# The MLP's two projections as units of 1024 cubed, each by seven half-size products, with GpSimd forming the operands' sums

## The chip, the core and the metric

The kernel runs on one core of a Trainium2 chip. The metric is the device time of one execution in microseconds (us), the median of three runs: 3414.43 us, with 3413.43 and 3418.71 as the other two. The engines are TensorE (PE; its weight loads are PEld), VectorE (DVE), ScalarE (ACT), GpSimd (POOL), and SyncE (SP), whose queue issues the DMA transfers. All data are float32.

## The reference, cut to what matters

Two transformer blocks run one after the other on 1024 tokens of width 1024. The change touches the very end, the squared-ReLU MLP of the second block, and the final norm only in its order:

```python
def squared_relu_mlp(xn, w_ff1, w_ff2):
    h = jax.nn.relu(jnp.einsum('bsd,df->bsf', xn, w_ff1))
    return jnp.einsum('bsf,fd->bsd', h * h, w_ff2)
...
        xn = rmsnorm(h, norm_mlp_g[l])
        h = h + squared_relu_mlp(xn, w_ff1[l], w_ff2[l])
    return rmsnorm(h, norm_final_g)
```

`xn` is 1024 x 1024, `w_ff1` 1024 x 4096, `w_ff2` 4096 x 1024: eight products of 1024 x 1024 by 1024 x 1024.

## The kernel before, in words

Every float32 matrix is cut in two parts: `high`, the value rounded to the format that TensorE multiplies (`F32R`), and `low`, the rest. A product is three matmuls, high x high, high x low and low x high; low x low is left out. A matmul is 128 x 128 by 128 x 512.

Each stage is one call of `project` (L462). It streams its weight through a `Stream` (L401): pieces of 128 x 2 x 512 (512 KB) are loaded to `m_w_raw` by SP (L427), ACT rounds each to its high part (L513), DVE subtracts for the low part (L517), both into `m_w_cut`, two pieces deep. A piece feeds eight PSUM tiles with six matmuls each (L626), 48 matmuls in all.

The MLP (`mlp_second`, L4112) takes the hidden width in eight chunks of 512. `up(j)` makes chunk j of the hidden layer from `mlp_high` and `mlp_low`, the normed rows, cut once for all chunks; ACT takes a PSUM tile with ReLU and squares it (L4134, L4135), DVE cuts it again (L4139, L4140). `down(j)` multiplies the chunk by its rows of `w_ff2`, and DVE adds the PSUM tile to `x` (L2022). The order is up(0), up(1), down(0), up(2), down(1), and so on: 3072 matmuls, 384 for each 1024-cubed product. While it goes on, GpSimd has nothing to do.

The stage ahead, `m2_out`, is a `project` too (128 x 3 matmuls). As it starts, SP loads the residual `x` (4 MB) and the gain vector, and behind them the third weight piece (`fetch`). At its end `RowsTurned` (L1401) norms rows 0 to 3: ACT squares and takes roots (L1432, L1435), DVE scales (L1446), PE transposes (L1452), ACT and DVE cut (L1457, L1461). Rows 4 to 7 follow between the first tiles of the MLP. At the end `FinalNorm` works in the same manner on each row tile as its last addition is done (L4179, L4202), and SP stores it.

What sets the order is each engine's own instruction list, with semaphores between them; engines also meet at the border of two stages.

## Time and profile before

| what | value |
|---|---|
| median of the runs | 3414.43 us (3413.43 to 3418.71) |
| span of the profiled execution | 3412.1 us |
| PE busy | 3092.3 us (91%), 14840 matmuls |
| DVE busy | 1392.4 us (41%) |
| ACT busy | 935.4 us (27%) |
| POOL busy | 188.4 us (6%) |
| share of the MLP's matmuls (L626, `mlp_ps`) in the chain that ended last | 20% |
| the MLP's matmuls, first and last start | 2698.0 and 3400.6 us |

The chain is followed back from the last instruction to what released each step. PE being busy says only that matmuls were in flight: whether it runs at its full rate is read from how far apart matmuls start and from the granted clock. Lines (L626) are those of the kernel before.

### The profile page before, as it was taken

The numbers are of one execution on the slowest core, as the hardware profiler recorded it, in microseconds if no ns is written. First come the engines' busy times: TensorE is split into PE (matmuls) and PEld (weight loads), VectorE is DVE, ScalarE is ACT, GpSimd is POOL, SyncE is SP. The second block draws the span as 40 slices with busy tenths as digits, with TensorE's granted clock in tenths as the row PEclk, the third lists the DMA queues.
The fourth block names the chain that finished last, engine by engine and source line by source line (L and its number), as shares of the span: only waits on it lengthen the run. The fifth ranks groups of instructions, "written<-read, shape, count | busy, mean of one in ns | idle before, by whom it ended". The sixth has DMA issues, their size and how long they took to land. (4 is left out here: it accounts for less than half of the span.)

```text
span 3412.1 us, 36355 instructions
## 1 busy us (share of the span) xinstructions
PE 3092.3 (91%) x14840; PEld 2322.7 (68%) x14840; DVE 1392.4 (41%) x2134; ACT 935.4 (27%) x1484; POOL 188.4 (6%) x247
## 2 busy tenths in 40 slices
PE   7997778999998888878774999999999999999998
PEld 7886754667776674322222977888887788888887
DVE  3126846884434343111115646521225433333334
ACT  3532335663324221000004131021321322222221
POOL 0001023110000001111112000000000000000000
PEclk9998889999999999998996999999999999999999
DMA  3111000003220048999995132111112121111112
GB/s 99 47 50 7 7 14 1 1 1 118 83 78 7 31 187 343 420 421 420 416 396 203 34 83 71 50 50 47 38 59 99 50 62 50 50 50 49 44 49 80
DMA packets 141158, 372.17 MB, mean 109 GB/s; under 512 B 45952, under 2 KB 59904, under 8 KB 115008
## 3 DMA queue, kind: packets, MB, share of 16 engines
q1 hardware_dynamic: 130640, 349.06, 28.3%
q0 software_dynamic: 9216, 16.80, 1.3%
q10 hardware_dynamic: 1152, 4.19, 0.3%
q8 instruction: 108, 1.77, 0.2%
q14 instruction: 42, 0.34, 0.0%
HBM read 354.80 MB, written 32.83 MB: 114 GB/s over the span
## 5 line engine op out<-in xcount | busy, mean ns | idle before, releaser
L517 DVE TENSOR_TENSOR m_w_cut<-m_w_raw,m_w_cut 128x1024 fp32r<-128x1024 f32 (+1 forms) x153 | 162.9, 1065 | 794.8 <-ACT m_w_cut L513 794.1
L513 ACT ACTIVATE m_w_cut<-m_w_raw 128x1024 fp32r<-128x1024 f32 (+1 forms) x153 | 142.3, 930 | 1010.5 <-PE mlp_ps L626 521.3
L626 PE MATMUL mlp_ps<-mlp_high,m_w_cut 128*128 128x512 f32 x1024 | 315.7, 390 | 1.1 <-PEq L572 1.1
L626 PE MATMUL mlp_ps<-m_w_cut,mlp_hidden_high 128*128 128x512 f32 x1024 | 315.2, 389 | 0.0
L2963 PE MATMUL ffn_ps<-moe_wgu,moe_rowsT 128*64 128x512 f32 x1024 | 240.0, 623 | 53.0 <-issue 26.5
L626 PEld LDWEIGHTS mlp_ps<-mlp_high,m_w_cut 128*128 128x128 f32 x1024 | 191.8, 188 | 40.9 <-issue 1.3
L626 PEld LDWEIGHTS mlp_ps<-m_w_cut,mlp_hidden_high 128*128 128x128 f32 x1024 | 192.2, 188 | 39.9
L2963 PEld LDWEIGHTS ffn_ps<-moe_wgu,moe_rowsT 128*64 128x64 f32 x1024 | 77.8, 143 | 194.6 <-issue 165.2
L626 PE MATMUL mlp_ps<-mlp_low,m_w_cut 128*128 128x512 f32 x512 | 199.2, 389 | 0.0
L626 PE MATMUL mlp_ps<-m_w_cut,mlp_hidden_low 128*128 128x512 f32 x512 | 199.2, 389 | 0.0
L2999 DVE TENSOR_TENSOR moe_hid<-ffn_ps,moe_gated 128x256 f32<-128x256 f32 x32 | 13.6, 425 | 414.5 <-ACT moe_gated L3011 414.5
L626 PE MATMUL m_cv_ps<-m_high,m_w_cut 128*128 128x512 f32 x512 | 162.4, 399 | 7.6 <-DVE m_w_cut L517 2.6
L626 PE MATMUL m_gates_ps<-m_high,m_w_cut 128*128 128x512 f32 x512 | 157.8, 389 | 1.1 <-PEq L572 1.1
L2984 PE MATMUL ffn_logitsT_ps<-moe_wd,moe_hidT 128*64 128x512 f32 x512 | 118.6, 605 | 18.0 <-DVE moe_hidT L3005 18.0
L626 PE MATMUL mix_in_ps<-mix_high,mix_w_cut 128*128 128x512 f32 x384 | 118.7, 390 | 0.1
L626 PEld LDWEIGHTS m_cv_ps<-m_high,m_w_cut 128*128 128x128 f32 x512 | 96.2, 191 | 31.0 <-DVE m_w_cut L517 7.7
L2022 DVE TENSOR_TENSOR x<-mlp_ps,x 128x512 f32<-128x512 f32 x128 | 86.9, 689 | 68.9 <-PE mlp_ps L626 68.9
L626 PEld LDWEIGHTS m_gates_ps<-m_high,m_w_cut 128*128 128x128 f32 x512 | 96.0, 188 | 21.3 <-issue 1.5
L626 PE MATMUL mix_in_ps<-mix_w_cut,mix_high 128*128 128x512 f32 (+1 forms) x384 | 109.6, 367 | 0.9 <-PEq L286 0.9
L626 PEld LDWEIGHTS mlp_ps<-mlp_low,m_w_cut 128*128 128x128 f32 x512 | 96.1, 188 | 20.0
L626 PEld LDWEIGHTS mlp_ps<-m_w_cut,mlp_hidden_low 128*128 128x128 f32 x512 | 96.1, 188 | 20.0
L517 DVE TENSOR_TENSOR mix_w_cut<-mix_w_raw,mix_w_cut 128x512 fp32r<-128x512 f32 (+1 forms) x47 | 31.4, 667 | 189.1 <-ACT mix_w_cut L513 189.0
(566 smaller groups left out, 5900.0 us busy)
## 6 DMA issues: line engine op xcount, KB each, us to landing
moe_wgu<-in_moe_w_gate_dram SPq DMA_DIRECT2D x64, 1024.0 KB, 20.0
moe_wgu<-in_moe_w_up_dram SPq DMA_DIRECT2D x64, 1024.0 KB, 25.3
moe_wd<-in_moe_w_down_dram SPq DMA_DIRECT2D x64, 1024.0 KB
m_w_raw<-in_w_ff_dram SPq DMA_DIRECT2D x68, 512.0 KB, 3.6
m_w_raw<-in_w_in_dram SPq DMA_DIRECT2D x48, 256.0 KB, 2.8
mix_w_raw<-in_w_in_dram SPq DMA_DIRECT2D x40, 256.0 KB, 2.6
m_w_raw<-in_w_in_dram SPq DMA_DIRECT2D x20, 512.0 KB, 3.6
x_w_raw<-in_x_w_kv_dram SPq DMA_DIRECT2D x16, 512.0 KB, 3.6
```

What stands on the lines that cost most here:

```text
L513: nc.scalar.activation(part(s, 0).bitcast(F32R), raw(s), ACT.Copy).then_inc(high_ready, 1)
L517: nc.vector.tensor_tensor(part(s, 1).bitcast(F32R), raw(s), part(s, 0), ALU.subtract).then_inc(low_ready, 1)
L626: ins = nc.tensor.matmul(ps[:, place, :r.shape[-1]], l, r, start=(k == 0 and sw is high and wh == 0), stop=(k == job.nk - 1 and sw is low))
L2022: return nc.vector.tensor_tensor(x[:, b, at], ps, x[:, b, at], ALU.add)
L2963: ins = self.nc.tensor.matmul(self.ps_h[r, i].rearrange("p (i n) -> p i n", i=2), self.rowsT[:, i, k, r], self.wgu[:, w * self.parts + h, ...
L2984: ins = self.nc.tensor.matmul(self.ps_y[r, half], self.hidT[:, i, k, r], self.wd[:, w * self.parts + h, k, half * CH:(half + 1) * CH], sta ...
L2999: self.nc.vector.tensor_tensor(self.hid[:, b % self.small], self.ps_h[:, b % self.small, EH:], self.gated[:, b % self.small], ALU.mult).th ...
```

## The change

The eight 1024-cubed products become eight `Unit`s in the order up 0, down 0, up 1, down 1, ... (an up unit makes 1024 hidden columns, a down unit adds its product to `x`). Each unit is done by the scheme of seven products of 512-cubed (Winograd's form of Strassen's). The operands A (activations) and B (weights) are taken as 2 x 2 blocks, and beside them four sums of each are formed:

- S1 = A21 + A22, S2 = S1 - A11, S4 = A12 - S2, S3 = A11 - A21
- T1 = B12 - B11, T2 = B22 - T1, T3 = B22 - B12, T4 = B21 - T2
- products in this order: A11 B11, A12 B21, S2 T2, S4 B22, S1 T1, S3 T3, A22 T4. They accumulate in two groups of four PSUM banks, and `TAKES` says to which of the four output blocks a bank's content is added after each product.

GpSimd makes the sums, 16 instructions of 128 x 1024 in a unit (each block in two halves). A product is two *pieces* g (its two halves in the contracted dimension), so 14 pieces in a unit and 112 in all; a piece is four PSUM tiles of six matmuls. Nothing is cut ahead of time any more: for every piece ACT rounds the A half and the B half (`high_a`, `high_w`), and DVE subtracts for the low parts (`low_a`, `low_w`, which read two operands in SBUF), into rings three pieces deep. ACT and DVE cut piece g+2 as soon as piece g-1 has been multiplied, and then take the PSUM tiles of piece g where it ends a product: in an up unit ACT copies the first content of a block and DVE adds the others (16 additions in a unit), in a down unit DVE makes all (32). ReLU and square run once a block is complete (`square`). The final norm of rows 0 to 3 moves into the last unit. The weight blocks lie in four slots of 1 MB; six half blocks are loaded in `m2_out` behind the residual, the B22 block of unit 0 only after row 7 has been turned, since its slot holds the rows' room until then.

```diff
@@ -4099,63 +4099,419 @@
-            mlp_jobs, mlp_rows, final, load_gain = mlp_second(c, a, x, base, flat(small))
+            mlp_rows, begin_mlp = mlp_second(c, a, x, base)
...
-            project(c, "mlp", stream, mlp_jobs, side=mlp_rows, tail=final)
+            mlp_rows.sevens.run()
+PRODUCTS = (("A11", "B11", 0, True), ("A12", "B21", 1, True), ("S2", "T2", 0, False), ("S4", "B22", 1, True),
+            ("S1", "T1", 0, False), ("S3", "T3", 1, True), ("A22", "T4", 1, False))
+TAKES = ((("11", True),), (("11", False),), (("21", True),), (("12", True),), (("12", False), ("22", True)),
+         (("22", False),), (("21", False),))
+SUMS = (("T1", 0), ("T2", 0), ("T1", 1), ("T2", 1), ("S1", 0), ("S2", 0), ("S1", 1), ("S2", 1),
+        ("S4", 0), ("S4", 1), ("T3", 0), ("S3", 0), ("T3", 1), ("S3", 1), ("T4", 0), ("T4", 1))
+USES = {name: q for q, names in enumerate(PRODUCTS) for name in names[:2]}
+FINAL = ("11", "12", "22", "21")
+SLOTS = {"B11": 0, "B21": 1, "B12": 2, "B22": 3, "T1": 0, "T2": 4, "T3": 2, "T4": 4}
+RING = 3
...
+    def high_a(self, act, g):
+        u, q, h = self.piece(g)
+        name = PRODUCTS[q][0]
+        if g >= RING:
+            act.wait_ge(self.products, 4 * (g - RING + 1))
+        if name[0] == "A":
+            self.act_ready(act, u, name, h)
+            src = self.a_block(u, name, h)
+        else:
+            act.wait_ge(self.summed, self.sum_done(u, name, h))
+            src = self.a_sum(name, h)
+        self.nc.scalar.activation(self.a_part(g, 0).bitcast(F32R), src, ACT.Copy).then_inc(self.a_high, 1)
...
+    def low_a(self, dve, g):
+        u, q, h = self.piece(g)
+        name = PRODUCTS[q][0]
+        src = self.a_block(u, name, h) if name[0] == "A" else self.a_sum(name, h)
+        dve.wait_ge(self.a_high, g + 1)
+        self.nc.vector.tensor_tensor(self.a_part(g, 1).bitcast(F32R), src, self.a_part(g, 0),
+                                     ALU.subtract).then_inc(self.a_low, 1)
...
+    def sum(self, pool, u, name, h):
+        nc = self.nc
+        out = self.w_slot(name, h) if name[0] == "T" else self.a_sum(name, h)
+        mine = lambda n: pool.wait_ge(self.summed, self.sum_done(u, n, h))
+        came = lambda n: pool.wait_ge(self.arrived[SLOTS[n]][h], 16 * (u + 1))
+        if name == "T1":
+            came("B12")
+            pool.wait_ge(self.w_low, self.split(u, "B11", h))
+            l, r = self.w_slot("B12", h), self.w_slot("B11", h)
+        elif name == "T2":
+            came("B22")
+            mine("T1")
+            if u:
+                pool.wait_ge(self.w_low, self.split(u - 1, "T4", h))
+            l, r = self.w_slot("B22", h), self.w_slot("T1", h)
+        elif name == "T3":
+            mine("T1")
+            l, r = self.w_slot("B22", h), self.w_slot("B12", h)
+        elif name == "T4":
+            mine("T2")
+            pool.wait_ge(self.w_low, self.split(u, "T2", h))
+            l, r = self.w_slot("B21", h), self.w_slot("T2", h)
+        elif name == "S1":
+            self.act_ready(pool, u, "A22", h)
+            self.act_ready(pool, u, "A21", h)
+            if u:
+                pool.wait_ge(self.a_low, self.split(u - 1, "S1", h))
+            l, r = self.a_block(u, "A21", h), self.a_block(u, "A22", h)
+        elif name == "S2":
+            mine("S1")
+            if u:
+                pool.wait_ge(self.a_low, self.split(u - 1, "S3", h))
+            l, r = self.a_sum("S1", h), self.a_block(u, "A11", h)
+        elif name == "S4":
+            mine("S2")
+            pool.wait_ge(self.a_low, self.split(u, "S2", h))
+            l, r = self.a_block(u, "A12", h), self.a_sum("S2", h)
+        else:
+            mine("S4")
+            pool.wait_ge(self.a_low, self.split(u, "S4", h))
+            l, r = self.a_block(u, "A11", h), self.a_block(u, "A21", h)
+        nc.gpsimd.tensor_tensor(out, l, r, ALU.add if name == "S1" else ALU.subtract).then_inc(self.summed, 1)
...
+        for block, first in TAKES[q]:
+            if (first and up) != (mine == "scalar"):
+                continue
+            for tile in range(4):
+                ps, at = self.ps[:, 4 * PRODUCTS[q][2] + tile], self.c_block(u, block, tile)
+                eng.wait_ge(self.products, 4 * g + tile + 1)
+                if mine == "scalar":
+                    if len(TAKES[q]) > 1:
+                        eng.wait_ge(self.added, adds + tile + 1)
+                    nc.scalar.activation(at, ps, ACT.Copy).then_inc(self.copied, 1)
+                    continue
...
+                nc.vector.tensor_tensor(at, ps, at, ALU.add).then_inc(self.added, 1)
...
+    def square(self, act, u, q):
...
+            self.nc.scalar.activation(at, at, ACT.Relu).then_inc(self.squared, 1)
+            act.wait_ge(self.squared, self.final_done(u, block, h))
+            self.nc.scalar.activation(at, at, ACT.Square).then_inc(self.made, 1)
...
+    def multiply(self, pe, g, tile):
+        u, q, h = self.piece(g)
+        _, _, banks, opens = PRODUCTS[q]
+        a, w = [[part(g, i).bitcast(F32R) for i in range(2)] for part in (self.a_part, self.w_part)]
+        if h == 0:
+            self.bank_free(pe, u, q, tile)
+        cols = slice(tile * P, (tile + 1) * P)
+        for k in range(2):
+            for n, (x, y) in enumerate(((0, 0), (0, 1), (1, 0))):
+                l, r = (w[y][:, k, cols], a[x][:, k]) if self.units[u].up else (a[x][:, k, cols], w[y][:, k])
+                ins = self.nc.tensor.matmul(self.ps[:, 4 * banks + tile], l, r, start=(opens and h == k == n == 0),
+                                            stop=(h == k == 1 and n == 2), skip_group_check=True)
+        ins.then_inc(self.products, 1)
+    def begin(self, sp):
+        for name in ("B11", "B21", "B12"):
+            for h in range(2):
+                self.load(sp, 0, name, h)
...
+                @block.sync
+                def _(sp):
+                    for u in range(len(units)):
+                        if u:
+                            for h in range(2):
+                                sp.wait_ge(self.w_low, self.split(u - 1, "T1", h))
+                                self.load(sp, u, "B11", h)
+                            for h in range(2):
+                                sp.wait_ge(self.summed, self.sum_done(u - 1, "T4", h))
+                                self.load(sp, u, "B21", h)
+                        else:
+                            sp.wait_ge(rows.turned, NT)
+                        for h in range(2):
+                            if u:
+                                sp.wait_ge(self.w_low, self.split(u - 1, "B22", h))
+                                sp.wait_ge(self.summed, self.sum_done(u - 1, "T3", h))
+                            self.load(sp, u, "B22", h)
+                        if u:
+                            for h in range(2):
+                                sp.wait_ge(self.w_low, self.split(u - 1, "T3", h))
+                                self.load(sp, u, "B12", h)
+                    final.last_stores(sp, self.a_low, 14 * last)
+                @block.gpsimd
+                def _(pool):
+                    c.clear()
+                    for u in range(len(units)):
+                        for name, h in SUMS:
+                            self.sum(pool, u, name, h)
+                @block.scalar
+                def _(act):
+                    self.high_a(act, 1)
+                    self.high_w(act, 1)
+                    for g in range(n):
+                        if g + 2 < n:
+                            self.high_a(act, g + 2)
+                            self.high_w(act, g + 2)
+                        for m in {0: (4, 5), 1: (6, 7)}.get(g, ()):
+                            rows.high(act, m)
+                        u, q, h = self.piece(g)
+                        if g and h == 0:
+                            u_was, q_was, _ = self.piece(g - 1)
+                            if units[u_was].up and any(not first for _, first in TAKES[q_was]):
+                                self.square(act, u_was, q_was)
+                        if h and units[u].up:
+                            self.take(act, u, q, "scalar")
+                        if u == last and q == 4 and h:
+                            final.roots(act, range(NT // 2), self.added, self.adds[self.at(u, 4)])
+                    final.roots(act, range(NT // 2, NT), self.added, self.adds[self.at(last, 6)] - NT // 2)
+                @block.vector
+                def _(dve):
+                    rows.scale(dve, 4)
+                    self.low_a(dve, 1)
+                    self.low_w(dve, 1)
+                    for g in range(n):
+                        if g == 0:
+                            rows.scale(dve, 5)
+                        if g + 2 < n:
+                            self.low_a(dve, g + 2)
+                            self.low_w(dve, g + 2)
+                        if g == 0:
+                            rows.scale(dve, 6)
+                            rows.scale(dve, 7)
+                        u, q, h = self.piece(g)
+                        if h:
+                            self.take(dve, u, q, "vector")
+                        if u == last and q == 5:
+                            for m in range(2 * h, 2 * h + 2):
+                                final.scale(dve, m)
+                    for m in range(NT // 2, NT):
+                        final.scale(dve, m)
+                @block.tensor
+                def _(pe):
+                    for g in range(n):
+                        pe.wait_ge(self.a_low, g + 1)
+                        pe.wait_ge(self.w_low, g + 1)
+                        if g == 2:
+                            pe.wait_ge(rows.split, NT)
+                        for tile in range(4):
+                            self.multiply(pe, g, tile)
+                            if tile in (1, 3) and g < 2:
+                                m = 4 + 2 * g + tile // 2
+                                if m >= 6:
+                                    pe.wait_ge(rows.split, m - 1)
+                                rows.turn_row(pe, m)
...
+    def beside_sums(self, act, added, before):
+        self.sevens.high_w(act, 0)
+        super().beside_sums(act, added, before)
+        self.sevens.high_a(act, 0)
+    def after_sum(self, dve, b):
+        if b is None:
+            self.scale(dve, 3)
+            self.sevens.low_w(dve, 0)
+            self.sevens.low_a(dve, 0)
+        elif 2 <= b < 5:
+            self.scale(dve, b - 2)
```

GpSimd's list, at the MLP. Before, the stage has only its branch; now the sums of each unit stand there (`mlp_raw` holds weight blocks, `mlp_sums` the S sums; the lines shown are unit 0).

```order
-L594 UNCONDITIONAL_BRANCH x2
+L594 UNCONDITIONAL_BRANCH
+L4392 UNCONDITIONAL_BRANCH
+L4285 TENSOR_TENSOR mlp_raw<-mlp_raw 128x1024 x4
+L4285 TENSOR_TENSOR mlp_sums<-mlp_normed 128x1024
+L4285 TENSOR_TENSOR mlp_sums<-mlp_sums,mlp_normed 128x1024
+L4285 TENSOR_TENSOR mlp_sums<-mlp_normed 128x1024
+L4285 TENSOR_TENSOR mlp_sums<-mlp_sums,mlp_normed 128x1024
+L4285 TENSOR_TENSOR mlp_sums<-mlp_normed,mlp_sums 128x1024 x2
```

The order is T1, T2, T1, T2, then S1, S2, S1, S2, S4, S4, and T3, S3, T3, S3, T4, T4 behind them.

VectorE's list in the MLP before: one subtraction for each weight piece, eight additions to `x` from PSUM for each down job, and the cut of the hidden tiles.

```order
L517 TENSOR_TENSOR m_w_cut<-m_w_raw,m_w_cut 128x1024 x4
L4139 CAST mlp_hidden_high_17665<-mlp_squares 128x512
L4140 TENSOR_TENSOR mlp_hidden_low_17666<-mlp_squares,mlp_hidden_high_17665 128x512
L2022 TENSOR_TENSOR x<-mlp_ps,x 128x512 x8
```

VectorE's list now, from a down unit's first additions on: pieces 3 and 4, then 5 and 6, and so on.

```order
L4313 TENSOR_TENSOR x<-mlp_ps,x 128x512 x4
L4235 TENSOR_TENSOR mlp_a_ring<-mlp_sums,mlp_a_ring 128x1024
L4241 TENSOR_TENSOR mlp_w_ring<-mlp_raw,mlp_w_ring 128x1024
L4235 TENSOR_TENSOR mlp_a_ring<-mlp_sums,mlp_a_ring 128x1024
L4241 TENSOR_TENSOR mlp_w_ring<-mlp_raw,mlp_w_ring 128x1024
L4313 TENSOR_TENSOR x<-mlp_ps,x 128x512 x4
```

The cut of the hidden tiles is gone, and two subtractions for each 24 matmuls have come in place of one for each 48.

TensorE's list now, from the start of the MLP.

```order
L4351 MATMUL mlp_ps<-mlp_a_ring,mlp_w_ring 128x512 x12
L1452 MATMUL mlp_ps<-ident,mlp_raw 128x128 x8
L4351 MATMUL mlp_ps<-mlp_a_ring,mlp_w_ring 128x512 x288
L4351 MATMUL mlp_ps<-mlp_w_ring,mlp_a_ring 128x512 x336
L4351 MATMUL mlp_ps<-mlp_a_ring,mlp_w_ring 128x512 x336
```

The first two of these lines stand there four times (rows 4 to 7); then follow the rest of unit 0 and the seven other units of 336 matmuls each.

## Rows read from the trace of the kernel before

**Rows 1.** The chain of waits from 2560 us on: start, duration, what.

```profile
2718.26 675.95 PE mlp_ps L626 x2982
```

**Rows 2.** Stretches: length, busy time of each engine (instructions), PE clock, DMA share, GB/s.

```profile
3000.00:3100.00 100.00, 100.00 (x443) 82.81 (x442) 36.15 (x50) 19.27 (x25) 0.00 (x0) 1.00 0.16 48
```

**Rows 3.** Timeline of PE at the MLP's end: start, duration, instruction.

```profile
3396.07 0.62 PE L626 MATMUL mlp_ps<-m_w_cut,mlp_hidden_high 128*128 128x512 f32 x2
...
3400.15 0.62 PE L626 MATMUL mlp_ps<-m_w_cut,mlp_hidden_high 128*128 128x512 f32 x2
```

**Rows 4.** Groups of instructions, 2600 to 3412 us: busy, mean ns; idle before.

```profile
L517 DVE TENSOR_TENSOR m_w_cut<-m_w_raw,m_w_cut 128x1024 fp32r<-128x1024 f32 x74 | 90.7, 1225 | 432.0 <-ACT m_w_cut L513 431.6
L2022 DVE TENSOR_TENSOR x<-mlp_ps,x 128x512 f32<-128x512 f32 x128 | 86.9, 689 | 68.9 <-PE mlp_ps L626 68.9
L513 ACT ACTIVATE m_w_cut<-m_w_raw 128x1024 fp32r<-128x1024 f32 x74 | 78.3, 1058 | 579.8 <-PE mlp_ps L626 521.3 <-PE m_out_ps L626 46.3 <-DMA m_w_raw<-in_w_out_dram 10.5
```

**Rows 5.** Timeline of POOL, 1825 to 1862 us.

```profile
1832.61 2.35 POOL L3259 TENSOR_TENSOR x<-x,m_t 128x1024 f32<-128x1024 f32 x1 [1.22 <-DVE x L3252]
...
1853.62 2.35 POOL L3259 TENSOR_TENSOR x<-x,m_t 128x1024 f32<-128x1024 f32 x1 [3.25 <-DVE x L3252]
```

**Rows 6.** Timeline of DVE in the same stretch.

```profile
1832.65 3.39 DVE L346 SCALAR_TENSOR_TENSOR m_t<-x,m_norm_rstd,m_t 128x1024 f32<-128x1024 f32 x1
...
1851.00 1.28 DVE L346 SCALAR_TENSOR_TENSOR m_t<-x,m_norm_rstd,m_t 128x1024 f32<-128x1024 f32 x1
...
1853.51 1.22 DVE L362 TENSOR_TENSOR m_low<-m_norm_ps,m_high 128x1024 fp32r<-128x1024 f32 x1
```

**Rows 7.** Timeline of POOL, 558 to 592 us.

```profile
561.50 2.33 POOL L907 TENSOR_TENSOR mla_k_low<-mla_kT,mla_k_high 96x1024 fp32r<-96x1024 f32 x1
571.99 1.30 POOL L903 TENSOR_TENSOR mla_q_low<-mla_qT,mla_attn_q_high 96x512 fp32r<-96x512 f32 x1 [8.17 <-ACT mla_attn_q_high L895]
573.25 2.81 POOL L907 TENSOR_TENSOR mla_k_low<-mla_kT,mla_k_high 96x1024 fp32r<-96x1024 f32 x1
```

**Rows 8.** Timeline of DVE in the same stretch.

```profile
572.47 1.38 DVE L983 TENSOR_SCALAR mla_attn_probs<-mla_attn_probs,mla_attn_inv 128x1024 f32<-128x1024 f32 x1
...
575.93 0.75 DVE L983 TENSOR_SCALAR mla_attn_probs<-mla_attn_probs,mla_attn_inv 128x1024 f32<-128x1024 f32 x1
```

**Rows 9.** Stretches at the start of `m2_out`, columns as in rows 2.

```profile
2596.00:2598.00 2.00, 0.00 (x0) 0.00 (x0) 1.97 (x3) 0.00 (x0) 0.00 (x0) 1.00 0.00 0
2598.00:2600.00 2.00, 1.67 (x5) 1.36 (x6) 1.04 (x3) 1.69 (x4) 0.00 (x0) 0.75 0.93 246
2600.00:2602.00 2.00, 2.00 (x6) 1.57 (x5) 2.00 (x5) 2.00 (x5) 0.00 (x0) 0.50 0.65 279
2602.00:2604.00 2.00, 2.00 (x9) 1.59 (x9) 2.00 (x5) 1.53 (x3) 0.00 (x0) 0.90 1.07 459
2606.00:2610.00 4.00, 4.00 (x19) 3.34 (x18) 0.00 (x0) 0.00 (x0) 0.00 (x0) 1.00 0.94 404
```

**Rows 10.** Timeline of ACT in `m2_out`: the third and fourth weight pieces.

```profile
2614.01 1.06 ACT L513 ACTIVATE m_w_cut<-m_w_raw 128x1024 fp32r<-128x1024 f32 x1 [10.48 <-DMA m_w_raw<-in_w_out_dram]
2622.09 1.06 ACT L513 ACTIVATE m_w_cut<-m_w_raw 128x1024 fp32r<-128x1024 f32 x1 [7.02 <-PE m_out_ps L626]
```

**Rows 11.** DMA issues, 2590 to 2700 us: KB each, median us to landing.

```profile
m_w_raw<-in_w_ff_dram SPq DMA_DIRECT2D x3, 512.0 KB, 3.6
```

**Rows 12.** Timeline, 2672 to 2730 us: around the start of the MLP.

```profile
2695.33 2.35 DVE L1461 TENSOR_TENSOR mlp_low<-m_out_ps,mlp_high 128x1024 fp32r<-128x1024 f32 x2 [1.05 <-ACT mlp_high L1457]
...
2698.01 0.70 PE L626 MATMUL mlp_ps<-mlp_high,m_w_cut 128*128 128x512 f32 x2 [1.11 <-PEq L572]
...
2701.82 1.09 PE L1452 MATMUL mlp_ps<-ident,mlp_squares 128*128 128x128 f32 x8 [0.83 <-DVE mlp_squares L1446]
```

**Rows 13.** Groups of instructions, 2600 to 3412 us: the turns in the MLP.

```profile
L1452 PE MATMUL mlp_ps<-ident,mlp_squares 128*128 128x128 f32 x32 | 4.2, 275 | 2.4 <-DVE mlp_squares L1446 2.4
```

**Rows 14.** Timeline of DVE at the end: the last scaling of a row.

```profile
3407.77 1.28 DVE L4202 SCALAR_TENSOR_TENSOR x<-x,s_small,fin_gain 128x1024 f32<-128x1024 f32 x1
```

192 lines of the change are left out of this document (146 added, 46 removed).

## The prediction

> **What bounds the kernel now.** I read the chain of waits first. From 2718.26 us on it is one piece, 675.95 us of the MLP's own matmuls [rows 1]: nothing else is waited for until the final norm. The table of stretches says the same: in 3000 to 3100 us PE is busy throughout at a granted clock of 1.00, with DVE busy 36, ACT 19, POOL 0 and the DMA engines 16% [rows 2]. How fast PE goes is read from the starts: 18 matmuls from 3396.07 to 3400.15 us, 0.2267 us each [rows 3]. So the MLP costs its number of matmuls times 0.2267 us, and everything else is cover. The change takes matmuls away and spends the cover; the question is whether the cover lasts. Times below are against the profiled span of 3412.1 us; the median of the runs is 2.3 us above it.
>
> **Matmuls removed.** 7 instead of 8 half-size products: 8 units x 14 pieces x 24 = 2688 matmuls instead of 3072. 384 x 0.2267 = 87.0 us less. A piece takes 24 x 0.2267 = 5.44 us, a unit 76.2 us. The form of the matmuls does not change.
>
> **What the other engines are given.** In a unit DVE has 28 subtractions at 1.225 us [rows 4] = 34.3 us and 16 additions (up) or 32 (down) at 0.689 [rows 4] = 11.0 or 22.0: 45 or 56 us of 76. ACT has 28 roundings at 1.058 us [rows 4], 30 us, and at most 16 ReLU and square instructions of the same size and 16 half-size copies, 56 us in an up unit. POOL has 16 sums; its nearest rows are the same instruction at the same size, 2.35 us [rows 5], so 37.6 us. Each engine alone fits into 76.2 us. Weight traffic stays the same.
>
> **But DVE and POOL are not alone.** A DVE instruction with two SBUF inputs that starts at 1832.65, 0.04 us behind a POOL sum of 2.35 us, lasts 3.39 us instead of the 1.28 of its like at 1851.00 [rows 5, 6]: it ends 1.08 us after the sum ends (1834.96), so it stood still for the sum's whole length. One whose first input is in PSUM keeps its 1.22 us beside the sum at 1853.62 [rows 5, 6]. So the 28 subtractions cannot run beside the 16 sums, while the additions can. Who comes next when both wait: POOL has two instructions back to back at 571.99 and 573.25; the DVE instruction issued at 572.47 lasts 1.38 us instead of 0.75 [rows 7, 8] and ends at 573.85, and POOL's second lasts 2.81 instead of 2.33, 0.48 longer. The waiter went in between. I take strict turns. The Trainium skill says this in "SBUF — State Buffer", section "Who interferes with whom": the port pair that both use is an exclusive lock for a whole instruction, and a DVE instruction with two SBUF inputs contends with a GpSimd one that reads SBUF. The trace agrees, with the 3.39 us. The skill also speaks against the placement ("GPSIMD Engine Reference", section "When to use GPSIMD": elementwise work on a tile belongs to VectorE); the trace's sum takes 2.35 us to DVE's 1.22 to 1.28.
>
> On the shared port a unit needs 28 x 1.08 + 16 x 2.35 = 68 us of 76.2: enough on average, not everywhere. I walk the lists, t = 0 where PE starts a unit, piece g due at 5.44 g. Cutting g+2 may begin at 5.44 g. POOL begins T1 at about -7 (it waits for the subtraction of B11), and the last of its 16 sums is bound only by its place in the list. With turns (low_a, sum, low_w, sum: 1.1 + 2.35 + 1.1 + 2.35 = 6.9 us for one piece) DVE loses about 1.5 us on each piece while POOL has a backlog. It starts with a lead of 10.9 - 3.5 = 7.4 us (two pieces, less the ACT and DVE time of a cut). In an up unit: piece 2 ready at 9, piece 3 at 16, 4 at 20.6 (due 21.8), 5 at 25.3, 6 at 32.3 (due 32.6), 7 at 39.2 (due 38.1), 8 at 46.2 (due 43.5), then POOL is through at 48.6 and DVE recovers. PE stands still 2.7 us. In a down unit DVE also has 4 additions behind pieces 3, 5 and 7, partly beside sums: piece 7 at 39.9, piece 8 at 49.3, 5.8 us of standstill. 4 x 2.7 + 4 x 5.8 = +34 us.
>
> Bounds: 0 if the sums fall beside additions and idle time (below nothing isn't possible, since a wait can't speed PE up). At the other end every sum delays DVE by its whole 2.35 us and DVE sets the pace: 34.3 + 11.0 + 37.6 = 82.9 and 34.3 + 22.0 + 37.6 = 93.9 us a unit against 76.2, 4 x 6.7 + 4 x 17.7 = 98 us. I keep 34, from the turns of rows 7 and 8.
>
> **The clock after a standstill.** At the start of `m2_out` PE has stood still for the 2.0 us of the first stretch (and a little at both sides); the clock then shows 0.75, 0.50 and 0.90 [rows 9], half level (1.2 GHz) for about 4 us, which costs 2 us. The gap of 1.1 us before the MLP [rows 12] is followed by matmuls at full rate. The long gap of each down unit (about 4 us at piece 8) is of the first kind: 4 x 2 = +8 us; bounds 0 and 16 (all eight units).
>
> **The start of the MLP.** The stage opens when `low_a(0)` is made. DVE's last work before was two cuts from 2695.33, ending at 2697.7 [rows 12]; now ACT rounds A11 behind its last row (+1.06) and DVE subtracts (+1.2), without those cuts: PE begins about 0.8 us later, 2698.8. Then 48 matmuls (10.9 us) and four turns (0.9 us each; [rows 12] has one with 1.09) bring it to 2713.4, and it waits about 1 us for row 7's copy. Here SP may first load B22: it lands 3.6 us later [rows 11], at 2717. T2 is second in POOL's list, so T2, T1, T2, S1, S2 run only from there: 5 x 2.35 = 11.8 us, 2729. Two roundings (2.1) and two subtractions with a sum between them (1.2 + 2.35 + 1.2) make piece 4 ready at 2736. PE has ended piece 3 at 2714.4 + 10.9 = 2725.3: 10.7 us of standstill, and 2 for the clock. Before, PE's waits in this stretch were 2.4 us [rows 13]. 0.8 + 1.0 + 10.7 + 2.0 - 2.4 = +12 us; bounds 6 (first S2 half at once, clock full) and 18.
>
> **`m2_out`.** The third weight piece is loaded behind the residual; ACT got it at 2614.01, and the fourth was released by PE at 2622.09 [rows 10], which is when PE turned to the third. Now 3 MB more lie in front: at the 404 GB/s of 2606 to 2610 [rows 9] 7.8 us, so it comes at 2621.8, is cut at 2624.1, and PE waits 2.0 us, with a little clock: +3 us, bounds 0 and 5.
>
> **The end.** Before, DVE's last scaling ends at 3409.05 [rows 14], 8.0 us after the last matmul (3400.15 + 0.62 + 0.23 = 3401.0), since eight rows are normed there. Now rows 0 to 3 are done before, and DVE has one addition and four scalings of 1.4 us left: 0.7 + 5.6 = 6.3 us. -1.7 us; the last store is the same.
>
> **Sum.** -87.0 + 34 + 8 + 12 + 3 - 1.7 = -32 us: span 3380, median 3382 us.
>
> **The rivals.**
>
> *The sums cost nothing.* POOL fits into DVE's idle half; the 68 of 76.2 us on the port speak for it, the lists' bunching (12 of 16 sums between t = 6 and 48) against it. Standstills and their clock go: -87 + 12 + 3 - 1.7 = -74 us, 3341 us. It would also come out if DVE's second subtraction always went ahead of a waiting sum.
>
> *Slower: DVE becomes the bound.* If a waiting sum goes first whenever it can, and the additions of down units are pushed behind it, the sums add to DVE's work in full: +98 for 34, -87 + 98 + 8 + 12 + 3 - 1.7 = +32 us, 3447 us. It decides from a standstill of (87 - 21) / 8 = 8.2 us a unit. For it: rows 5 and 6, DVE loses the whole length. Against it: it asks that no addition and no idle time ever lies beside a sum, with DVE idle 20 to 31 us of a unit.
>
> *The saving is eaten exactly.* Standstills of 6 to 9 us in both kinds of units, with half clock behind each: -87 + 60 + 16 + 12 + 3 - 2 = +2 us, 3416 us.
>
> **How the numbers follow.** Forecast with its neighbourhood (3358 to 3404) 0.62; sums free 0.20; eaten 0.10, half of it within 0.2%; slower 0.08. 0.2% (6.8 us) is about what a measurement of this kernel can tell from no change. From these: faster 0.85, same 0.05, slower 0.10. The range takes in most of the free case and reaches to the eaten one: 3341 to 3412.
>
> **What would show it.** Right: 2688 matmuls at 0.227 us with PE standing still around pieces 7 and 8 of each unit, longer in down units, waiting for a DVE subtraction; subtractions of 3.4 to 3.6 us beside the usual 1.2; sums of 2.35 us or, behind a subtraction, up to 3.5; one standstill of about 10 us at piece 4 of unit 0, with T2 waiting for a DMA; additions with 0.69 us throughout. Wrong: subtractions that keep 1.2 us beside sums (then the free case), several sums in a row while one subtraction stands (then the slower one), PE waiting for ACT or for a DMA in the later units, or matmuls further apart than 0.227 us without a wait.

## The result, and the profile after

The changed kernel takes 3377.93 us (median of four runs, 3375.55 to 3384.36); the kernel before, on the same chip, 3416.57 us (3413.43 to 3419.94; four runs, with the three known ahead of the prediction among them). The ratio is 0.989, 95% interval 0.9876 to 0.9904: 1.1% faster. The forecast was 3382.0 us, the interval 3341 to 3412. The profiled span is 3373.8 us, against 3412.1.

Where the change acts is measured better between marks of the trace than by spans, since where `m2_out` begins moves by 16 us between executions of kernels that are equal up to there (2593 to 2609 us).

| stretch (us) | before | after | difference | forecast |
|---|---|---|---|---|
| first matmul of `m2_out` to first of the MLP | 99.7 | 103.0 | +3.3 | +3.8 |
| first to last matmul of the MLP | 703.0 | 668.2 | -34.8 | -33.8 |
| last matmul to the end | 11.1 | 9.4 | -1.7 | -1.7 |
| together | 813.8 | 780.6 | -33.2 | -32 |

The other 5.1 us of the span's difference lie ahead of `m2_out`, where nothing was changed. The +3.8 is the +3 of `m2_out` and the 0.8 by which the MLP was to begin later.

The groups of instructions from 2600 us on (busy, mean ns, idle before with its releasers), against [rows 4]:

```profile
L4351 PE MATMUL mlp_ps<-mlp_w_ring,mlp_a_ring 128*128 128x512 f32 x1344 | 316.3, 397 | 18.3 <-issue 13.1 <-DVE mlp_w_ring L4241 2.7 <-DVE x L4313 2.5
L4351 PE MATMUL mlp_ps<-mlp_a_ring,mlp_w_ring 128*128 128x512 f32 x1344 | 313.1, 393 | 21.2 <-issue 13.9 <-DVE mlp_hidden L4313 2.4 <-PEq L572 2.4
L4241 DVE TENSOR_TENSOR mlp_w_ring<-mlp_raw,mlp_w_ring 128x1024 fp32r<-128x1024 f32 x112 | 219.6, 1961 | 0.0
L4285 POOL TENSOR_TENSOR mlp_raw<-mlp_raw 128x1024 f32<-128x1024 f32 x64 | 178.6, 2797 | 892.0 <-POOLq L572 671.0 <-DVE mlp_w_ring L4241 201.1 <-DMA mlp_raw<-in_w_ff_dram 17.9
L4313 DVE TENSOR_TENSOR x<-mlp_ps,x 128x512 f32<-128x512 f32 x128 | 79.8, 679 | 6.0 <-PE mlp_ps L4351 6.0
```

There are 2688 matmuls. The same subtraction that took 1225 ns takes 1961 on average. The T sums (into `mlp_raw`) take 2797 instead of 2350, the S sums 3140 to 3354, and the additions out of PSUM keep their 0.68 us. PE stands still 39.5 us, mostly called "issue": there the semaphores don't show whom it waits for, so the engines' own timelines must. PE in the down unit of the second pair of units, against [rows 2], where it never stopped:

```profile
2955.76 38.24 PE L4351 MATMUL mlp_ps<-mlp_w_ring,mlp_a_ring 128*128 128x512 f32 x168
2994.69 5.68 PE L4351 MATMUL mlp_ps<-mlp_w_ring,mlp_a_ring 128*128 128x512 f32 x24 [0.69 <-DVE mlp_w_ring L4241]
3003.65 4.57 PE L4351 MATMUL mlp_ps<-mlp_w_ring,mlp_a_ring 128*128 128x512 f32 x12 [3.28 <-issue]
```

168 matmuls are seven pieces, then piece 7 is late by 0.69 us, and piece 8 by 3.28. DVE at that time:

```profile
2987.78 3.42 DVE L4235 TENSOR_TENSOR mlp_a_ring<-mlp_sums,mlp_a_ring 128x1024 fp32r<-128x1024 f32 x1
2991.13 3.42 DVE L4241 TENSOR_TENSOR mlp_w_ring<-mlp_raw,mlp_w_ring 128x1024 fp32r<-128x1024 f32 x1
2994.47 2.47 DVE L4313 TENSOR_TENSOR x<-mlp_ps,x 128x512 f32<-128x512 f32 x4
2996.86 3.39 DVE L4235 TENSOR_TENSOR mlp_a_ring<-mlp_sums,mlp_a_ring 128x1024 fp32r<-128x1024 f32 x1
3000.18 3.37 DVE L4241 TENSOR_TENSOR mlp_w_ring<-mlp_raw,mlp_w_ring 128x1024 fp32r<-128x1024 f32 x1
3003.48 1.21 DVE L4235 TENSOR_TENSOR mlp_a_ring<-mlp_sums,mlp_a_ring 128x1024 fp32r<-128x1024 f32 x1
```

And POOL:

```profile
2990.09 3.37 POOL L4285 TENSOR_TENSOR mlp_raw<-mlp_raw 128x1024 f32<-128x1024 f32 x1
2993.43 3.39 POOL L4285 TENSOR_TENSOR mlp_sums<-mlp_hidden 128x1024 f32<-128x1024 f32 x1
2996.76 5.70 POOL L4285 TENSOR_TENSOR mlp_raw<-mlp_raw 128x1024 f32<-128x1024 f32 x2
```

Piece 8 starts when the subtraction at 3000.18 ends (3003.55). While both have work, each instruction of either lasts its own time and the other's (1.08 + 2.3 = 3.4 us): strict turns, as [rows 7, 8] had it. The four additions at 2994.47, out of PSUM, keep 2.47 us beside a sum. The moment POOL's list is empty (3002.46) the subtractions are back at 1.21. The clock behind the standstill (columns as in [rows 2]), against [rows 9]:

```profile
3002.00:3004.00 2.00, 0.35 (x2) 0.34 (x3) 2.00 (x2) 0.42 (x1) 0.47 (x1) 1.00 0.00 0
3004.00:3006.00 2.00, 2.00 (x7) 1.57 (x6) 2.00 (x3) 0.00 (x0) 0.00 (x0) 0.56 0.51 150
3006.00:3008.00 2.00, 2.00 (x7) 1.58 (x6) 2.00 (x4) 0.00 (x0) 0.00 (x0) 0.58 0.67 185
3008.00:3010.00 2.00, 2.00 (x10) 1.63 (x10) 2.00 (x3) 0.00 (x0) 0.00 (x0) 1.00 1.01 359
```

The first twelve matmuls take 4.57 us; at the full clock it would be 12 x 0.2267 and 0.17 for the last one's overlap, 2.9: 1.7 us lost. The other down units have the same standstill of 3.28 us at piece 8, but not always the same clock behind it. The stretch of unit 1 that lies 3.6 to 5.6 us behind its piece 8 (2841.40) is still at half level, its like of unit 3 is nearly over it:

```profile
2845.00:2847.00 2.00, 2.00 (x6) 1.60 (x5) 2.00 (x3) 0.00 (x0) 0.00 (x0) 0.50 0.82 275
3007.00:3009.00 2.00, 2.00 (x9) 1.55 (x9) 2.00 (x4) 0.00 (x0) 0.00 (x0) 0.83 0.73 226
```

Behind 2841.40, 70 matmuls take 18.86 us, 2.8 more than at the full clock; behind 3325.87, 96 take 24.86, 2.9 more; units 3 and 5 lose 1.7 each. PE around the start of the MLP, against [rows 12, 13], and at its end:

```profile
2696.23 4.58 PE L4351 MATMUL mlp_ps<-mlp_a_ring,mlp_w_ring 128*128 128x512 f32 x12 [2.37 <-PEq L572]
...
2713.76 11.16 PE L4351 MATMUL mlp_ps<-mlp_a_ring,mlp_w_ring 128*128 128x512 f32 x48 [1.21 <-ACT mlp_normed L4467]
2735.18 4.99 PE L4351 MATMUL mlp_ps<-mlp_a_ring,mlp_w_ring 128*128 128x512 f32 x15 [10.26 <-issue]
...
3353.26 11.13 PE L4351 MATMUL mlp_ps<-mlp_w_ring,mlp_a_ring 128*128 128x512 f32 x48 [2.54 <-DVE x L4313]
```

The 10.26 us are the first standstill forecast (10.7). What lies behind them, in the timeline of all engines (B22's loads; T2, T1, T2; the first S2; piece 4's first rounding):

```profile
2712.58 0.88 SPq L4195 DMA_DIRECT2D mlp_raw<-in_w_ff_dram  x2
2716.40 7.26 POOL L4285 TENSOR_TENSOR mlp_raw<-mlp_raw 128x1024 f32<-128x1024 f32 x3 [17.89 <-DMA mlp_raw<-in_w_ff_dram]
2726.07 2.34 POOL L4285 TENSOR_TENSOR mlp_sums<-mlp_sums,mlp_normed 128x1024 f32<-128x1024 f32 x1
2728.50 1.06 ACT L4216 ACTIVATE mlp_a_ring<-mlp_sums 128x1024 fp32r<-128x1024 f32 x1 [12.93 <-POOL mlp_sums L4285]
```

POOL waits for B22, then five sums follow one another. PE also waits at piece 12 of each up unit, for PSUM banks. Here is DVE, and then PE, in unit 2:

```profile
2941.66 1.22 DVE L4235 TENSOR_TENSOR mlp_a_ring<-mlp_normed,mlp_a_ring 128x1024 fp32r<-128x1024 f32 x1 [3.61 <-ACT mlp_a_ring L4216]
2943.93 2.47 DVE L4313 TENSOR_TENSOR mlp_hidden<-mlp_ps,mlp_hidden 128x512 f32<-128x512 f32 x4
2944.76 11.16 PE L4351 MATMUL mlp_ps<-mlp_a_ring,mlp_w_ring 128*128 128x512 f32 x48 [0.60 <-DVE mlp_hidden L4313]
```

The additions that free the banks stand behind piece 13's cut in DVE's list, and that cut has waited 3.61 us for ACT, which does ReLU and square from 2936.49 to 2940.67 before it rounds.

### The profile page after: what moved, and what is told of

Same layout as the page of the kernel before. It is cut to its first block and busy times, and to the rows that moved or that the text cites. A ratio compares the mean times of both kernels' runs of the same rounds, so it can differ in the third digit from the quotient of the medians.

```text
span 3373.8 us, 36498 instructions
## 1 busy us (share of the span) xinstructions
PE 3018.7 (89%) x14456; PEld 2254.7 (67%) x14456; DVE 1725.5 (51%) x2218; ACT 1108.4 (33%) x1640; POOL 578.7 (17%) x375
## 5 line engine op out<-in xcount | busy, mean ns | idle before, releaser
L4351 PE MATMUL mlp_ps<-mlp_w_ring,mlp_a_ring 128*128 128x512 f32 x1344 | 316.3, 397 | 18.3 <-issue 13.1
L4351 PE MATMUL mlp_ps<-mlp_a_ring,mlp_w_ring 128*128 128x512 f32 x1344 | 313.1, 393 | 21.2 <-issue 13.9
L4285 POOL TENSOR_TENSOR mlp_raw<-mlp_raw 128x1024 f32<-128x1024 f32 x64 | 178.6, 2797 | 892.0 <-POOLq L572 671.0
L4351 PEld LDWEIGHTS mlp_ps<-mlp_w_ring,mlp_a_ring 128*128 128x128 f32 x1344 | 257.9, 193 | 76.1 <-issue 21.9
L4351 PEld LDWEIGHTS mlp_ps<-mlp_a_ring,mlp_w_ring 128*128 128x128 f32 x1344 | 253.0, 189 | 79.0 <-issue 24.1
L517 DVE TENSOR_TENSOR m_w_cut<-m_w_raw,m_w_cut 128x512 fp32r<-128x512 f32 (+1 forms) x86 | 80.8, 940 | 414.0 <-ACT m_w_cut L513 413.6
L513 ACT ACTIVATE m_w_cut<-m_w_raw 128x512 fp32r<-128x512 f32 (+1 forms) x86 | 71.4, 830 | 490.4 <-PE m_gates_ps L626 190.7
L4241 DVE TENSOR_TENSOR mlp_w_ring<-mlp_raw,mlp_w_ring 128x1024 fp32r<-128x1024 f32 x112 | 219.6, 1961 | 0.0
L4235 DVE TENSOR_TENSOR mlp_a_ring<-mlp_sums,mlp_a_ring 128x1024 fp32r<-128x1024 f32 x64 | 162.6, 2540 | 29.5 <-ACT mlp_a_ring L4216 28.3
L4227 ACT ACTIVATE mlp_w_ring<-mlp_raw 128x1024 fp32r<-128x1024 f32 x112 | 117.1, 1045 | 0.0
```

Source lines behind the costliest of these rows:

```text
L513: nc.scalar.activation(part(s, 0).bitcast(F32R), raw(s), ACT.Copy).then_inc(high_ready, 1)
L517: nc.vector.tensor_tensor(part(s, 1).bitcast(F32R), raw(s), part(s, 0), ALU.subtract).then_inc(low_ready, 1)
L4227: self.nc.scalar.activation(self.w_part(g, 0).bitcast(F32R), self.w_slot(name, h), ACT.Copy).then_inc(self.w_high, 1)
L4235: self.nc.vector.tensor_tensor(self.a_part(g, 1).bitcast(F32R), src, self.a_part(g, 0), ALU.subtract).then_inc(self.a_low, 1)
L4241: self.nc.vector.tensor_tensor(self.w_part(g, 1).bitcast(F32R), self.w_slot(PRODUCTS[q][1], h), self.w_part(g, 0), ALU.subtract).then_inc( ...
L4285: nc.gpsimd.tensor_tensor(out, l, r, ALU.add if name == "S1" else ALU.subtract).then_inc(self.summed, 1)
```

## The experiments

"MLP" below is the stretch from its first to its last matmul in the profiled execution: 703.0 us before, 668.2 after.

**1. Do the sums cost DVE time by reading SBUF, or only by being work for GpSimd?** In the place of each sum GpSimd fills two tiles, 1.17 and 0.96 us, reading nothing. The sums are left out.

```diff
-        nc.gpsimd.tensor_tensor(out, l, r, ALU.add if name == "S1" else ALU.subtract).then_inc(self.summed, 1)
+        self.fill(nc.gpsimd.memset(self.filler[:], 0.0))
+        nc.gpsimd.memset(out, 0.0).then_inc(self.summed, 1)
```

> Each of GpSimd's 128 sums is replaced by two memsets (a spare 128 x 1280 room, then the sum's place), which only write; the sums themselves are left out, so S and T are zero. GpSimd should stay about as busy (some 2.2 us for each) and every semaphore stays. Theory A (the shared read port, as in the prediction): the subtractions of VectorE keep 1.22 us throughout, PE's gaps at pieces 7 and 8 of the units vanish, from the first MLP matmul to the last 668 us become about 633, the time about 3343 us; the gap at piece 4 of unit 0 stays at 8 to 10 us, since it hangs on B22's arrival and five GpSimd steps. Rival B (the length of GpSimd's chain of sums holds PE, whatever they read): gaps stay, 3378 us. Rival C (VectorE's own load is too high without any blocking): gaps stay as well, with subtractions of 1.22 us.

Measured: 3341.8 us (3338.5 to 3348.8), ratio 0.9781 (0.9755 to 0.9806), MLP 631.6 us. Groups of DVE and of POOL from 2700 us on:

```profile
L4242 DVE TENSOR_TENSOR mlp_w_ring<-mlp_raw,mlp_w_ring 128x1024 fp32r<-128x1024 f32 x111 | 135.3, 1219 | 0.0
```

```profile
L4286 POOL MEMSET mlp_filler<- 128x1280 f32 x128 | 149.7, 1170 | 984.6 <-POOLq L572 674.0 <-DVE mlp_w_ring L4242 236.9 <-DVE mlp_a_ring L4236 48.5
```

The subtractions keep 1219 ns beside 272 us of GpSimd's writing, and the standstills at pieces 7 and 8 are gone. So it is the sums that cost it, and not GpSimd being busy or its chain of waits; that it is their reading is the one thing the fills don't share with them, apart from the kind of instruction. At piece 4 of unit 0 PE stands still 6.03 us, not the 8 to 10 expected: the fills are shorter, and the cuts beside them are not held up.

**2. The same from the other side:** from unit 1 on, each sum covers 2 of 512 columns.

```diff
+        few = slice(0, 2 if u else CH)
+        nc.gpsimd.tensor_tensor(out[:, :, few], l[:, :, few], r[:, :, few],
+                                ALU.add if name == "S1" else ALU.subtract).then_inc(self.summed, 1)
```

> From unit 1 on each sum covers only 2 of its 512 columns (the rest of every sum is left out); unit 0 is untouched. Theory A: the same as with writes only, within 3 us, gaps of units 1 to 7 gone, about 3345 us; unit 0's 10.3 us gap stays. Rival B: this one is faster (about 3345), while the one with writes only is not. Rival C: gaps stay, 3378 us.

Measured: 3347.0 us (3345.7 to 3354.6), 0.9802 (0.9778 to 0.9825), MLP 637.6. Unit 0 keeps its 10.18 us at piece 4; units 1 to 7 keep only the waits that are not the sums':

```profile
2735.98 4.60 PE L4353 MATMUL mlp_ps<-mlp_a_ring,mlp_w_ring 128*128 128x512 f32 x10 [10.18 <-issue]
...
2936.49 3.67 PE L4353 MATMUL mlp_ps<-mlp_a_ring,mlp_w_ring 128*128 128x512 f32 x15 [0.61 <-DVE mlp_hidden L4315]
...
3242.90 11.16 PE L4353 MATMUL mlp_ps<-mlp_a_ring,mlp_w_ring 128*128 128x512 f32 x48 [0.61 <-DVE mlp_hidden L4315]
3321.88 12.78 PE L4353 MATMUL mlp_ps<-mlp_w_ring,mlp_a_ring 128*128 128x512 f32 x48 [2.54 <-DVE x L4315]
```

A pair of units takes 153.2 us, against 161.1 in the changed kernel (piece 8 of its down units starts at 2841.40, 3003.65, 3164.79 and 3325.87; the first pair has 162.3): 7.9 us a pair is what the sums cost, with the half clock behind their standstills. Since S and T are wrong or zero in these two runs, it matters that experiment 7, with every sum right, has the same 153.2 us.

**3. The last six sums of a unit spread over later pieces.**

```diff
+PACE = {("T3", 0): 6, ("S3", 0): 7, ("T3", 1): 8, ("S3", 1): 9, ("T4", 0): 9, ("T4", 1): 10}
...
+        pace = PACE.get((name, h))
+        if pace is not None:
+            pool.wait_ge(self.w_low, 14 * u + pace + 1)
```

> Nothing is left out. The last six sums of a unit are held back, so that they spread over pieces 6 to 10 instead of following at once. Theory A with bunching (the port is full only while GpSimd has a backlog): the gaps at pieces 7 and 8 shrink by two thirds or more, the half clock behind those of down units goes, 20 to 26 us less than the changed kernel, about 3354 us. Rival D (the amount of sums is too much for a unit, wherever they stand): the standstill moves to later pieces, within 5 us of 3378.

Measured: 3364.3 us (3363.7 to 3372.9), 0.9854 (0.9829 to 0.9878), MLP 652.0. A miss by 10 us. The standstills at pieces 7 and 8 went, and another came:

```profile
2944.02 12.76 PE L4355 MATMUL mlp_ps<-mlp_a_ring,mlp_w_ring 128*128 128x512 f32 x48 [2.73 <-DVE mlp_hidden L4317]
...
3339.94 12.74 PE L4355 MATMUL mlp_ps<-mlp_w_ring,mlp_a_ring 128*128 128x512 f32 x48 [4.00 <-DVE x L4317]
```

Piece 12 reuses the PSUM banks that DVE empties behind piece 11 (`bank_free`). In unit 2 the cuts at 2922.99 and 2927.45 us last 3.4 us each beside a late sum, so the additions behind piece 9 begin late (2930.79). ACT's copies, ReLU and squares follow them, then the cut of piece 13 (3.61 us of waiting for ACT), and only then the additions that free the banks. I had watched only the cuts.

**4. T1, S1, S2 ahead of T2 in GpSimd's list.**

```diff
-SUMS = (("T1", 0), ("T2", 0), ("T1", 1), ("T2", 1), ("S1", 0), ("S2", 0), ("S1", 1), ("S2", 1),
+SUMS = (("T1", 0), ("T1", 1), ("S1", 0), ("S2", 0), ("T2", 0), ("S1", 1), ("S2", 1), ("T2", 1),
```

> Nothing is left out. GpSimd's list begins T1, T1, S1, S2, T2, S1, S2, T2 instead of T1, T2, T1, T2, S1, S2, S1, S2. Theory A: in unit 0 only T2 waits for B22, so S2's first half is ready at about 2718.3 and T2's at 2720.7 instead of S2's at 2728.4: the 10.3 us gap at piece 4 becomes 2 to 3 us and the half clock after it may go, 8 to 10 us less, about 3369 us; the other units keep 161 us a pair. Rival E (the gap is the row tail itself, ACT's copies and the cut, not the order): less than 3 us change.

Measured: 3385.6 us (3380.1 to 3391.6), 0.9902 (0.9877 to 0.9928), MLP 669.8. A miss. Piece 4 does start 30.8 us after the MLP's start instead of 39.0, but the turning of rows 4 and 5 waits 0.45 and 2.00 us. The 0.45 is in experiment 3 too, where the first twelve matmuls also ran at the full clock; the 2.00 comes from DVE's scaling of row 5, 3.43 us instead of 1.28, beside a T1 sum that in the changed kernel's list waits for B22. And then:

```profile
2741.45 5.71 PE L4351 MATMUL mlp_ps<-mlp_a_ring,mlp_w_ring 128*128 128x512 f32 x24 [0.61 <-issue]
2750.45 12.59 PE L4351 MATMUL mlp_ps<-mlp_a_ring,mlp_w_ring 128*128 128x512 f32 x48 [3.30 <-DVE mlp_w_ring L4241]
2763.96 5.69 PE L4351 MATMUL mlp_ps<-mlp_a_ring,mlp_w_ring 128*128 128x512 f32 x24 [0.92 <-DVE mlp_w_ring L4241]
```

Piece 8 comes 59.9 us after the start, instead of 63.7, and the later units, with the same sums in another order, stand 1.09 + 1.00 + 3.24 us (down) and 0.84 + 0.92 (up). The gain at piece 4 was given back, and more.

**5. The changed kernel once more, and its six first loads behind the third weight piece of `m2_out`.**

> The changed kernel once more, as the yardstick of this call: 3378 us, 161 us for a pair of units, ratio 0.989 to the kernel before.

```diff
                     stream.load(sp, s, pieces[s][2])
+                    if s == 2 and fetch_late:
+                        fetch_late(sp)
```

> Nothing is left out. The six weight loads for the MLP are issued behind m2_out's third weight piece instead of ahead of it. Theory A (the 3 MB in front of the piece make PE wait): the 2.4 to 2.9 us gap at the third piece of m2_out goes, 2 to 3 us less than the changed kernel; the MLP itself is unchanged. Rival (the piece is late for another reason, or the fourth piece now waits behind the 3 MB): no change, or the gap one piece later.

Measured: 3379.4 us (3376.3 to 3383.8), 0.9892 (0.9872 to 0.9912), and 3376.2 (3373.1 to 3378.8), 0.9888 (0.9867 to 0.9909). From the first matmul of `m2_out` to the MLP: 102.7 and 99.8 us (103.0 after, 99.7 before). The 3 us are clear between marks; the medians lie 3.1 apart with ranges that overlap.

**6. The S sums on VectorE, or all sixteen.** DVE makes the sums named at the places `AFTER` gives.

```diff
+ON_VECTOR = ("S1", "S2", "S3", "S4")
+AFTER = {1: (("S1", 0), ("S2", 0)), 2: (("S1", 1), ("S2", 1)), 3: (("S4", 0),), 4: (("S4", 1),),
+         7: (("S3", 0),), 8: (("S3", 1),)}
...
+        eng = nc.vector if name in ON_VECTOR else nc.gpsimd
```

> Nothing is left out. The eight S sums of a unit are made by VectorE (about 1.2 us each) at fixed places of its list, the eight T sums stay with GpSimd. Theory A (a sum on GpSimd costs VectorE up to 2.35 us of standing still, one on VectorE 1.2 us of work): a down unit is at most 34.3 + 22 + 9.8 + 18.8 = 85 us instead of 94, the gaps at pieces 7 and 8 shrink by two thirds, 15 to 25 us less than the changed kernel, about 3357 us. Rival F (VectorE is the scarce engine, and giving it more work makes it later): gaps grow, 3390 us or more.

> Nothing is left out. All 16 sums of a unit are made by VectorE, GpSimd does nothing. Theory A: no subtraction lasts longer than 1.23 us; VectorE has 45.3 + 19.6 = 65 us in an up unit and 76 in a down unit of 76.2, so up units have no gaps and down units small ones; 20 to 33 us less than the changed kernel, about 3352 us. Rival F: down units are then bound by VectorE, with order and waits some us above its 76 us of work each, 3375 us or more.

With all sixteen the order is also another: it begins T1, T1, S1, S2, T2, as in experiment 4, each at its place in `AFTER`. Measured: S on DVE 3383.7 us (3380.1 to 3388.4), 0.9912 (0.9891 to 0.9934), MLP 671.8, a miss: no better than all on GpSimd. PE stands still at other pieces: 0.77 and 2.34 us at pieces 4 and 5 of a down unit, 0.98, 1.45 and 0.31 at 5 to 7 of an up unit, and 0.4 to 1.0 at piece 12. DVE ahead of the 2.34, at piece 5:

```profile
2976.50 3.31 DVE L4295 TENSOR_TENSOR mlp_sums<-mlp_sums,mlp_hidden 128x1024 f32<-128x1024 f32 x1
2980.99 1.23 DVE L4244 TENSOR_TENSOR mlp_a_ring<-mlp_sums,mlp_a_ring 128x1024 fp32r<-128x1024 f32 x1 [1.19 <-ACT mlp_a_ring L4225]
```

The S2 sum is now itself held up by a T sum on GpSimd (3.31 us), and behind it DVE stands idle for 1.19 us while ACT rounds it: a sum on DVE just ahead of its own cut costs 1.22 us and this wait. All on DVE 3362.5 (3356.4 to 3367.2), 0.9845 (0.9821 to 0.9869), MLP 647.2, 10 above its forecast. With all sixteen every DVE instruction is back at 1.22 us, and nothing is late at pieces 4, 7 or 8, but:

```profile
2934.68 5.50 PE L4362 MATMUL mlp_ps<-mlp_a_ring,mlp_w_ring 128*128 128x512 f32 x23 [0.60 <-DVE mlp_hidden L4324]
3014.93 0.77 PE L4362 MATMUL mlp_ps<-mlp_w_ring,mlp_a_ring 128*128 128x512 f32 x1 [3.81 <-DVE x L4324]
```

Piece 12 of a down unit waits 3.81 us for its banks: DVE has 34.3 + 22 + 16 x 1.22 = 76 us of work there, all of the 76.2, and waits 1.19 us for ACT behind each S2 besides. The last unit waits 7.69 us. A pair takes 158.6 to 158.9 us.

**7. Twelve sums on VectorE, and GpSimd's four (T3, T4) released where DVE turns to its additions out of PSUM.** Then with the loads of experiment 5 and a later final scaling; and that scaling alone.

```diff
+ON_VECTOR = ("S1", "S2", "S3", "S4", "T1", "T2")
+AFTER = {0: (("T1", 0), ("T1", 1)), 1: (("S1", 0), ("S2", 0), ("T2", 0)), 2: (("S1", 1), ("S2", 1), ("T2", 1)),
+         3: (("S4", 0),), 4: (("S4", 1),), 5: (("S3", 0),), 6: (("S3", 1),)}
+PACE = {("T3", 0): 5, ("T3", 1): 7, ("T4", 0): 11, ("T4", 1): 11}
...
-                        if u == last and q == 5:
-                            for m in range(2 * h, 2 * h + 2):
+                        if u == last and q == 6 and not h:
+                            for m in range(NT // 2):
```

> VectorE makes twelve of the sixteen sums of a unit (S1, S2, S4, S3, T1, T2), GpSimd only T3 and T4, each released by the cut after which VectorE turns to additions out of PSUM (pieces 5, 7 and 11). My theory: a GpSimd sum costs VectorE nothing while VectorE adds out of PSUM, and VectorE then has 28 x 1.22 + 12 x 1.22 + 32 x 0.68 = 71 us of work in a down unit of 76. The standstills at pieces 7, 8 and 12 go (below 1 us each), a pair of units takes 153 to 154 us against 158.9 with all sums on VectorE, and the time is 3362.5 - 4 x 5.4 = 3341 us, 3336 to 3348. Rival, a GpSimd sum costs VectorE its 2.35 us wherever it lies: 71 + 4 x 2.35 = 80 us in a down unit, 3.5 us above TensorE's 76.2, a pair of 157 us and 3355 us. Rival, the wait for q5's additions at piece 12 stays, as in both earlier tries: 3360 us.

> The kernel above, with the six first weight loads behind the third piece of m2_out and with the final scaling of rows 0 to 3 moved behind the last addition of product 6 in the last unit (VectorE has nothing else to do there). Expected: 3 us from the loads (seen once already) and 2.5 us from the standstill before the last product, so 5.5 us below the kernel above: 3336 us, 3330 to 3344, if my theory of that one holds. If VectorE's scalings then come late at the end (6.3 us behind the last matmul becomes more), the second 2.5 us go.

> The changed kernel, with the final scaling of rows 0 to 3 in the last unit moved from product 6's to product 7's first piece. Theory: the 2.54 us of standstill before the last product are the wait for PSUM banks that VectorE empties late, because two scalings lie ahead of the additions; they go, and the time is 2 to 4 us shorter, 3375 us. Rival: the additions are late through the earlier turns with GpSimd; then the standstill stays and nothing changes.

Measured: 3343.6 us (3334.7 to 3347.0), 0.9784 (0.9768 to 0.9799), MLP 624.2; combined 3328.7 (3324.8 to 3333.1), 0.9752 (0.9738 to 0.9765), MLP 618.1; scaling alone 3378.7 (3377.1 to 3380.4), 0.9897 (0.9881 to 0.9912), MLP 664.0. The first came as forecast (a pair takes 153.2 us). The combined kernel came out 14.9 us below it where 5.5 were forecast, and 1.3 below the range. Between the marks 2.8 us are the loads (102.6 to 99.8) and 6.0 the MLP; of these 6.0, 2.7 are the standstill before the last product, and 3.3 are clock: the first one's standstills of 2.37 and 2.54 us are followed by half level, 1.6 to 1.7 us each. The spans differ by 9.5 more ahead of `m2_out`, where nothing was changed. The scaling alone did what it says inside the MLP (no standstill before the last product; 4.2 us less, 2.7 of them by that; about 1.1 are clock behind piece 8 of the down units, 8.0 us in all against 9.1), and its median does not show it: its `m2_out` began at 2600.7 us, against 2593.2. The combined kernel on POOL, in the down unit:

```profile
2958.78 2.41 POOL L4301 TENSOR_TENSOR mlp_raw<-mlp_raw 128x1024 f32<-128x1024 f32 x1 [43.54 <-DVE mlp_w_ring L4253]
2970.58 2.42 POOL L4301 TENSOR_TENSOR mlp_raw<-mlp_raw 128x1024 f32<-128x1024 f32 x1 [9.39 <-DVE mlp_w_ring L4253]
2987.48 4.78 POOL L4301 TENSOR_TENSOR mlp_raw<-mlp_raw 128x1024 f32<-128x1024 f32 x2 [14.48 <-DVE mlp_w_ring L4253]
```

On DVE beside the second of them:

```profile
2969.28 1.22 DVE L4253 TENSOR_TENSOR mlp_w_ring<-mlp_raw,mlp_w_ring 128x1024 fp32r<-128x1024 f32 x1
2970.42 2.48 DVE L4329 TENSOR_TENSOR x<-mlp_ps,x 128x512 f32<-128x512 f32 x4
2972.81 1.26 DVE L4301 TENSOR_TENSOR mlp_sums<-mlp_hidden 128x1024 f32<-128x1024 f32 x1
```

The sum lies beside four additions, and neither engine waits. In up units one of the four still meets a cut (3.32 us at 3045.09). In 3000 to 3100 us:

```profile
3000.00:3100.00 100.00, 99.39 (x439) 81.97 (x438) 75.97 (x77) 60.60 (x68) 10.50 (x4) 1.00 0.13 45
```

That is [rows 2] again, with an eighth of the matmuls gone.

**8. The combined kernel without the waits of `PACE`:** the same four sums, as early as their operands allow.

```diff
-        pace = PACE.get((name, h))
-        if pace is not None:
-            pool.wait_ge(self.w_low, 14 * u + pace + 1)
         if name == "T1":
...
         elif name == "T3":
+            came("B22")
```

> The best kernel so far (twelve sums on VectorE, T3 and T4 on GpSimd, late loads, late scaling; 3328.7 us) without the waits that hold GpSimd's four sums until VectorE adds out of PSUM: they run as soon as their operands are there, T3 beside the first cuts and sums of a unit. It tells what did the work: fewer sums on GpSimd, or where they lie. If each of the four now costs VectorE its 2.35 us, a down unit asks 71 + 9.4 = 80 us of VectorE against 76.2, a few us of standstill in each down unit come back, and the time is 8 to 16 us longer, 3337 to 3345 us. Rival: VectorE has enough lead (one lead of 7.4 us a unit) to take four, and only their number counted; then it is 3329 us as with the waits.

Measured: 3355.8 us (3349.2 to 3358.6), 0.9821 (0.9806 to 0.9836), MLP 645.6: 27 us longer, where 8 to 16 were forecast.

```profile
2977.64 5.71 PE L4364 MATMUL mlp_ps<-mlp_w_ring,mlp_a_ring 128*128 128x512 f32 x24 [1.75 <-DVE mlp_w_ring L4252]
2984.77 0.47 PE L4364 MATMUL mlp_ps<-mlp_w_ring,mlp_a_ring 128*128 128x512 f32 x1 [1.43 <-issue]
```

DVE has, ahead of these, a subtraction of 3.41 us and an S2 sum of 3.31 us, each beside one of the four. Where GpSimd's sums lie counts for as much as how many there are.

## Why the prediction was right, step by step

- **Matmuls, -87.0:** right. 2688, and 168 of them in 38.24 us (0.227 each).
- **Standstills and the clock behind them, +34 and +8:** the mechanism was right (turns on a shared path, pieces 7 and 8, longer in down units); the size of the standstills was too large. Measured: 4 x 7.9 = 31.6 us, and 2.3 more for the longer half level in the first and the last down unit, 33.9 for 42. The walk had the up unit late by 2.7 and the down unit by 5.8; the brackets have 0.36 + 0.92 and 0.69 + 3.28 (each standstill costs about 0.2 more, since the bracket counts from the end of a matmul that overlaps the next). Piece 8 of the down unit was to be ready 49.3 us after the unit's start and came after 3003.65 - 2955.76 = 47.9. From piece 6 on the walk took every cut to meet a waiting sum. In the trace POOL pauses 1.23 us twice in this unit (S4 needs S2's cut), and the subtraction of that moment takes 1.21. The clock costs 2.8, 1.7, 1.7 and 2.9 us behind the four standstills of 3.28, 9.1 for the 8 forecast, and nothing behind the 0.92; so the standstills alone are 25 us for 34.
- **Start of the MLP, +12:** the 0.8 us of a later start came as a standstill of 2.37 instead of 1.11. Inside the MLP 11.2 us were forecast: read are 10.26 at piece 4 (10.7), 1.21 for row 7 (1.0), 0.4 of overlap, 1.4 of clock behind piece 4's wait and, not foreseen, 1.6 behind the 2.37 (twelve matmuls in 4.58 us), less the 2.4 of before: 12.5.
- **`m2_out`, +3:** right in place and size: the third piece's wait is 2.88 us (2.0 and a little clock), and experiment 5 takes 3 us back.
- **The end, -1.7:** right.
- **Not foreseen:** two waits for PSUM banks. Piece 12 of each up unit waits 0.61 us (4 x 0.8 = 3.2 us with the overlap), and the last product 2.54 us (2.7), since two final scalings stand ahead of DVE's additions (experiment 10 takes it away). Inside the MLP this makes -87 + 33.9 + 12.5 + 3.2 + 2.7 = -34.7, against the measured -34.8. So the standstills with their clock were over-sized by 8 us, and the two bank waits (5.9) and a start 1.3 us dearer took 7 of it back: that the total inside the MLP comes out within 1 us is partly luck.
- **The rivals:** with sums that cost nothing the time is 3347.0 us (experiment 2, unit 0 as it was) or 3341.8 (experiment 1, where the start is 4 us cheaper too), and the rival had 3341: priced a few us low, without the bank waits. It did not happen, because the sums hold the cuts up. DVE as the bound did not happen with the sums on GpSimd; it did, in down units, with all sixteen on DVE. A subtraction takes 3.4 us beside a sum and 1.219 beside a fill, and an addition out of PSUM keeps its 0.68. The Trainium skill's "SBUF — State Buffer", section "Who interferes with whom", says that a DVE instruction with two SBUF inputs contends with a GpSimd one that reads SBUF, and not with one that only writes: borne out both ways. A sum on DVE costs DVE 1.22 us, one on GpSimd 2.2 us beside cuts, and all sixteen on DVE are 17 us faster than all on GpSimd. This agrees with the Trainium skill's "GPSIMD Engine Reference", section "When to use GPSIMD", which gives elementwise work on a tile to VectorE; but the eight S sums alone on DVE gained nothing (3383.7). It holds by place: beside additions out of PSUM the GpSimd sum costs nothing, and four of them there, with S3 now ahead of T3, are worth 19 us against all on DVE (3362.5 to 3343.6; 23 inside the MLP).

## What to carry to other kernels

A GpSimd operation with two SBUF inputs takes its length from a VectorE that has two SBUF inputs too, and the two engines alternate; an idle GpSimd is free cover only beside VectorE's work out of PSUM or beside its idle time, and a semaphore can put it there. Walk the cuts, but walk also who empties the PSUM banks, and whom that engine's list waits for first: two of the misses above (experiment 3, and all sixteen sums on DVE in experiment 6) were a bank wait a product later. When one product is bought out of eight, it is worth 87 us only where all the others' cover holds: the changed kernel gains 39 of them, the combined one 85.

## What was not expected of the hardware

- A standstill of about 2.4 us at the start of the MLP is followed by the half clock in some executions and not in others: the first twelve matmuls take 4.58 us after 2.37 (the changed kernel), and 2.99 after the same 2.37 (the combined kernel). Of the 13 profiled executions with this standstill nine have the half clock there (4.2 to 4.6 us for the twelve matmuls). So it is at piece 8 of the down units: the same 3.28 us are followed by 1.7 to 2.9 us of loss in the changed kernel, and when it ran once more, the first of the four by none (84 matmuls in 19.29 us). What decides stays open, and some us between two executions hang on it.
- Waiting works in both directions: GpSimd's sums last up to 3.43 us beside VectorE's cuts and 2.34 without. GpSimd's fills, which only write, cost VectorE's cuts nothing (1219 ns, and 1.22 us with GpSimd idle in experiment 6).
